# Head-by-head query scores and early best-sixteen lists in a retention, sparse-attention and expert-lookup layer, with gate products from the 24th expert block

## The reference

```python
q = (xt @ wq).reshape(n, 8, 2, 128)                 # 8 heads, 2 sides
s = einsum('nhpd,pkd->nhpk', q, subkeys)            # 128 scores for each head and side
sv, si = top_k(s, 16)
cand = sv[:, :, 0, :, None] + sv[:, :, 1, None, :]  # 16 x 16 sums
cs, ci = top_k(cand.reshape(n, 8, 256), 16)
eidx, gate = ..., softmax(cs)                       # 16 experts of a head, of 128*128
hid = gelu(einsum('cd,chkd->chk', x, u[eidx]))
out = einsum('chk,chkd->cd', gate * hid, v[eidx])
```

## Time and profile before

| | us |
|---|---|
| median of 3 runs (1794.49 to 1795.36) | 1794.93 |
| the profiled execution, its span | 1793.2 |
| TensorE busy in the span | 1774.3 (99%) |
| VectorE busy | 1388.5 (77%) |
| ScalarE busy | 766.7 (43%) |
| GpSimd busy | 170.8 (10%) |

### The profile page before, as it was taken

One profiled execution on the slowest core, in us unless ns is written; L12 is line 12 of the kernel. 1 busy time (PEld: TensorE's weight loads), 2 busy tenths in 40 slices (PEclk: granted clock), 3 DMA queues, 4 the chain that ended last, 5 costly groups with the idle time before them and its releaser, 6 DMA issues.

```text
span 1793.2 us, 27943 instructions
## 1 busy us (share of the span) xinstructions
PE 1774.3 (99%) x10680; PEld 1591.7 (89%) x10680; DVE 1388.5 (77%) x2153; ACT 766.7 (43%) x1054; POOL 170.8 (10%) x158
## 2 busy tenths in 40 slices
PE   8999999999999999999999999999999999999998
PEld 8899989789999999999977777789999998777775
DVE  6546667566459796888378898989999998898996
ACT  5334444655331010111155555555555555555555
POOL 0000000000000121222100000111111111111010
PEclk9999999999999999999999999999999999999999
DMA  9774544556545987998999899999999999999984
GB/s 351 262 280 149 165 141 142 188 187 226 187 150 192 358 333 282 342 336 331 362 377 361 317 324 341 344 350 367 377 369 374 377 347 361 353 359 365 357 309 152
DMA packets 77275, 531.01 MB, mean 296 GB/s; under 512 B 8811, under 2 KB 9211, under 8 KB 16268
## 3 DMA queue, kind: packets, MB, share of 16 engines
q1 hardware_dynamic: 54512, 377.96, 56.6%
q0 software_dynamic: 22352, 151.59, 23.2%
q10 hardware_dynamic: 332, 0.44, 0.1%
HBM read 512.60 MB, written 15.20 MB: 294 GB/s over the span
## 4 chain that ended last, share of the span: by engine, by line
PE 97%; DVE 1%; issue 1%; ACT 1%; DMA 0%; DVEq 0%; SPq 0%; ACTq 0%
PE bank L918 19%; PE bank L934 11%; PE bank L596 8%; PE bank L597 8%; PE bank L598 8%; PE bank L1015 6%; PE bank L1014 6%; PE bank L1019 6%; PE bank L1021 6%; PE bank L1020 6%; PE bank L935 5%; PE bank L973 2%; PE bank L743 0%; PE bank L952 0%; PE bank L791 0%
## 5 line engine op out<-in xcount | busy, mean ns | idle before, releaser
L1932 DVE TENSOR_TENSOR lo<-raw,hi 128x1024 fp32r<-128x1024 f32 x384 | 463.6, 1221 | 101.7 <-ACT hi L1318 101.3
L1318 ACT ACTIVATE hi<-raw 128x1024 fp32r<-128x1024 f32 x384 | 404.9, 1059 | 320.8 <-PE bank L1021 233.5
L918 PE MATMUL bank<-hT,raw 128*128 128x192 f32 x2048 | 337.4, 326 | 0.0
L918 PEld LDWEIGHTS bank<-hT,raw 128*128 128x128 f32 x2048 | 332.3, 190 | 0.1
L934 PE MATMUL bank<-xr,hi 128*128 128x384 f32 x1024 | 291.3, 359 | 0.0
L935 PE MATMUL bank<-xr,lo 128*128 128x192 f32 x1024 | 256.3, 250 | 0.0
L1444 DVE TENSOR_TENSOR lo<-raw,hi 128x2048 fp32r<-128x2048 f32 x75 | 171.8, 2290 | 103.7 <-ACT hi L1086 68.2
L1015 PE MATMUL bank<-lo,wm 128*64 128x512 f32 x512 | 202.8, 396 | 0.0
L1014 PE MATMUL bank<-hi,wm 128*128 128x512 f32 x512 | 199.9, 390 | 1.7 <-DVE wm L1987 1.2
L1019 PE MATMUL bank<-lo,wm 128*128 128x512 f32 x512 | 200.3, 391 | 0.0
L1021 PE MATMUL bank<-hi,wm 128*128 128x512 f32 x512 | 199.3, 389 | 0.0
(11 more groups left out here) (293 smaller groups left out, 2686.2 us busy)
## 6 DMA issues: line engine op xcount, KB each, us to landing
raw<-in_u SPq DMA_DIRECT2D x128, 1024.0 KB, 7.7
raw<-in_v SPq DMA_DIRECT2D x128, 1024.0 KB, 7.2
raw<-in_w_in SPq DMA_DIRECT2D x43, 1024.0 KB, 5.8
raw<-in_w_out SPq DMA_DIRECT2D x16, 1024.0 KB, 4.8
raw<-in_wq SPq DMA_DIRECT2D x16, 1024.0 KB, 4.8
gate_matrix<-gs POOLq DMA_DIRECT2D x12, 768.0 KB, 12.5
gs<-gate_matrix SPq DMA_DIRECT2D x12, 768.0 KB, 9.2
raw<-in_cmp_w SPq DMA_DIRECT2D x8, 1024.0 KB, 4.8
```

The costliest lines, as they stand in the source:

```text
L918: last = mm(bank[s % 2][:, 0:TD], raw[:, s, k * P:(k + 1) * P], xn[:, k, 0:TD], start=(k == 0), stop=(k == KT - 1))
L1318: do(hi[:, s % 2, cols], raw[:, s, cols], ACT.Copy).then_inc(v_hi_ready, 1)
L1932: vec.tensor_tensor(lo[:, n % 2, cols], raw[:, n % RAW, cols], hi[:, n % 2, cols].bitcast(F32), ALU.subtract).then_inc(v_lo_ready, 1)
```

## The change

**Scores.** `query_scores(h)` makes the four products of one head (both sides, both halves of the tokens) behind block 2h + 2 of the query stage, into bank 2 or 3. Heads 0 to 6 are made there, head 7 behind `u` block 0, where all eight were. ScalarE copies a head's scores with one instruction, `copy_scores(h)`, behind its rounding of block 2h + 4.

**Lists.** `early_list()` makes one list at a time. VectorE does 20 of them (heads 0 to 4, both sides, both halves) in the query stage: one in block 4, two in each of the blocks 5 to 11, one in each of the blocks 12 to 15, and one more behind them. `route_tokens` keeps the lists of heads 5 to 7.

**Gates.** `ROUTED` goes from 32 to 24: TensorE waits for the choices after `u` block 23, gate products lie in the blocks 25 to 48, 24 expert columns are gated at once and 104 are stored, in 13 groups. The first 14 items are let through from block 9 on and are shared over 13 parts of tt = 0 (before: 18), the next 24 lie in the blocks 24 to 59 (before: 32 to 59).

**Places.** `sc` moves to `gs`, the sums and the wide passes to `arena`, the lists to a tile `top_sb` of their own. The loops over the query blocks are written out on TensorE, ScalarE and VectorE.

```diff
-ROUTED = 32
+ROUTED = 24
+EARLY_HEADS = 5
...
-EXP_SPARSE, EXP_DENSE, PAIRS_LISTED = 10, 27, 13
+EXP_SPARSE, EXP_DENSE, PAIRS_LISTED = 7, 20, 9
...
+            def query_scores(h):
+
+                if h == 0:
+                    pe.wait_ge(decay_loaded, 32)
+                if h >= 2:
+                    pe.wait_ge(q_copied, h - 1)
+                pe.wait_ge(acc_evacuated, M_WQ + 2 * h + 2)
+                for tt in range(2):
+                    for s in range(2):
+                        g, to = 2 * h + s, (2 * tt + s) * P
+                        last = mm(bank[2 + h % 2][:, to:to + P], qT[:, g * T + tt * P:g * T + (tt + 1) * P], subk[:, s, :], start=True, stop=True)
+                last.then_inc(q_scores, 1)
+
+            for b in range(2, KT):
+                weights_block(M_WQ + b, b, x=h_parts)
+                if b % 2 == 0:
+                    query_scores(b // 2 - 1)
...
+            for b in range(RAW, KT):
+                rest_block(M_WQ + b, b, b % RAW)
+                if RAW < b < KT - RAW:
+                    early_list()
+                scaled(M_WQ + b - 1, b - 1, qT[:, (b - 1) * T:b * T])
+                if b >= KT - RAW:
...
+                early_list()
+            while done["lists"] < 4 * EARLY_HEADS:
+                early_list()
+            scaled(M_PEER - 1, 1, qT[:, (KT - 1) * T:KT * T])
...
-                total = PH + PH // 2 + 6
+                total = PH - EARLY_HEADS + PH // 2 + 6
...
-                for x in range(PH):
+                for x in range(EARLY_HEADS, PH):
                     g = 2 * x
-                    dv.wait_ge(q_copied, 4 * (1 - tt) + x // 2 + 1)
+                    dv.wait_ge(q_copied, x + 1)
```

More of the change, by code:

```diff
@@ L217, in build @@
         choiceT = at("choiceT", 50432, [P, 3, T])
+        top_sb = at("top_sb", 49152, [P, 2, 512])
         base = at("base", 51200, [P, 3 * P + 3 * TS])
@@ L944, in _ @@
                 if r == 0:
[L945 to L954, removed]
+                    query_scores(PH - 1)
             with pe.Fori(1, ROUTED // RAW) as lap:
@@ L1298, in pair_gelus @@
                     do(cols, cols, ACT.Gelu_apprx_tanh).then_inc(hcol_ready, 1)
[L1300 to L1303, removed]
+            for h in range(PH - 2, PH):
+                copy_scores(h)
             ac.wait_ge(res_stored, 16)
@@ L1758, in _ @@
                 normalise((0, 8)[s - 2], (8, KT)[s - 2])
[L1759 to L1774, removed]
+            done = {"route": 0, "items": 0, "lists": 0}
             def step(ins):
@@ L1783, in routed, with best16, early_list @@
                 dv.wait_ge(route, done["route"])
+            def best16(vals, idx, src):
+                for v, l in zip(vals, src):
+                    step(vec.max(v[:, 0:8], l))
+                routed()
+                for v, x, l in zip(vals, idx, src):
+                    step(vec.max_index(x[:, 0:8], v[:, 0:8], l))
+                routed()
+                for v, l in zip(vals, src):
+                    step(vec.match_replace(l, v[:, 0:8], l, LOWEST))
+                routed()
+                for v, l in zip(vals, src):
+                    step(vec.max(v[:, 8:16], l))
+                routed()
+                for v, x, l in zip(vals, idx, src):
+                    step(vec.max_index(x[:, 8:16], v[:, 8:16], l))
+                routed()
+            def early_list():
+                n = done["lists"]
+                done["lists"] += 1
+                h, tt, s = n // 4, 1 - n % 4 // 2, n % 2
+                g = 2 * h + s
+                dv.wait_ge(q_copied, h + 1)
+                best16([top[:, tt, g, :]], [top_i[:, tt, g, :]], [sc[:, tt, g, :]])
+            for b in range(RAW, KT):
+                rest_block(M_WQ + b, b, b % RAW)
[3 more added lines that the diff above has]
+                if b >= KT - RAW:
+                    if b == KT - RAW:
+                        dv.wait_ge(sparse_loaded, 16)
+                        dv.wait_ge(rstd_ready, 3)
+                    s = b - KT + RAW
+                    cols = slice(s * 512, (s + 1) * 512)
+                    vec.scalar_tensor_tensor(out=xs[TS:P, cols], in0=h_sparse[:, cols], scalar=rstd_cols[TS:P, 1:2], in1=g2_row[TS:P, cols],
+                                             op0=ALU.mult, op1=ALU.mult).then_inc(xs_ready, 1)
+                early_list()
+            while done["lists"] < 4 * EARLY_HEADS:
+                early_list()
+            scaled(M_PEER - 1, 1, qT[:, (KT - 1) * T:KT * T])
             def pair_item():
```

45 lines of the change are left out of this document (12 added, 33 removed).

## The result

| | kernel before | changed kernel |
|---|---|---|
| median, us | 1794.71 (1794.22 to 1795.36, 4 runs) | 1813.67 (1812.42 to 1814.47, 4 runs) |
| span of the profiled execution, us | 1793.2 | 1812.0 |

The ratio is 1.0105, with a 95% interval of 1.0093 to 1.0116: the changed kernel is slower by 19 us. Forecast were 14.8 us and a time of 1809.7; the measured time lies inside the range, 1801 to 1817, and the other side of the forecast (TensorE waits for the choices) came about. The 4.2 us between forecast and loss are mainly two terms: a wait 2.6 us longer, and 2.1 us behind it that the sum did not have. The sum's 0.4 us for the first `v` stage did not come about.

What follows compares the result with a forecast made beforehand. TensorE, busy 99% of the span, was taken as the bound. To the median of 1794.9 us came 14.4 us of waiting for the choices, 0 for the query stage and 0.4 for the first `v` stage: 1809.7 us, range 1801 to 1817.

Steps and rivals of the forecast that it cites:

- 0.4 us for the first `v` stage: First `v` stage: eight more blocks gated just ahead of use cost TensorE 0.4 us, bounds 0 and 4.1.
- TensorE arrives at the transposes: End of `u` block 23: TensorE reaches the transposes of the choices at about 648.0 us.
- cost of the query stage: Query stage: VectorE's early lists fit beside the blocks, so TensorE waits 0 us, bounds 0 to 3.7.
- pairs leave: End of the tt = 1 lists: pairs leave for GpSimd at 569.0 us, 14.9 us earlier than before.
- item 0 / item 2 / item 7: VectorE's gathered tiles in tt = 0: multiplications start at 579.6, 591.6 and 625.7 us.
- item 11 / item 13: Last gathered tiles: two row buffers yield one per 6.0 us; item 13 starts at 659.3 us.
- choices ready: End of VectorE's routing: 3.1 us from the last tile's start to the choices, at 662.4 us.
- wait: Ahead of the transposes: TensorE stands 14.4 us for the choices; 9 to 22 us expected, chance 72%.
- the landing of the last gathers: Gathers ahead of the choices: 8.9 us from issue to multiplication, the last about 6.5 us without weight loads.
- The forecast by the Trainium skill's rule: Gathers at an estimated 4.4 us per 1 MB: stall about 4.5 us, time 1800; the prediction went by the rows instead.
- The rival of an overrun: Query stage: single lists of 2.1 us make VectorE overrun, 3.7 us more, 1813.4 us; chance 7%.
- The signs: Expected in the trace: VectorE idle some 7 us before its first tile, query blocks 5.76 and 6.65, choices 24 to 27 earlier.
- The choices come in time: At the choices: added gather waits shrink under 3 us, TensorE does not stand, 1794.9 to 1798 us; chance 7%.

Runs made afterwards that it cites:

- experiment 1: Changed kernel with ROUTED back at 32 and the exponentials and pair lists at their old values, leaving head-by-head scores and early lists: 1794.47 us, ratio 1.0.
- experiment 5: Changed kernel with a third row buffer for the first fourteen gathered tiles and the last two of them multiplied behind the choices: 1794.90 us, ratio 1.0001.
- experiment 7: Changed kernel with 140 more transposes of a constant tile, results unused, on TensorE ahead of its wait for the choices: 1810.78 us.
- experiment 2: Kernel before with only the gates moved to block 24 and the exponentials to blocks 10 and 23, no early lists: 1831.51 us, one run.
- experiment 8: Kernel of experiment 1 with two more searches, results overwritten, ahead of each of the twenty early lists: 1805.95 us, ratio 1.0063.
- two tiles behind: Changed kernel with the last two of the fourteen gathered tiles multiplied behind the choices, all gathers left in place: 1804.85 us, ratio 1.0051.
- experiment 3: Changed kernel with a third row buffer for the first fourteen gathered tiles, nothing else changed: 1804.15 us, ratio 1.0052.

## Why the prediction was right, point by point

The mechanism, its place and its sign were right. The size was 4.2 us short, and by luck no more: VectorE's lead of 1.4 us at item 7 and the 0.4 us for the `v` stage, both misjudged, worked against the two errors below. Without them 6.0 us would have been missing. What each step gave:

| step | forecast, us | measured, us |
|---|---|---|
| TensorE arrives at the transposes | 648.0 | 648.0 (665.02 - 17.01) |
| single list in the query stage | 1.82 | 1.83 |
| cost of the query stage | 0 | 0 (experiment 1) |
| pairs leave | 569.0 | 568.3 |
| item 0 / item 2 / item 7 | 579.6 / 591.6 / 625.7 | 578.5 / 589.6 / 624.3 |
| item 11 / item 13 | 649.7 / 659.3 | 651.0 / 661.9 |
| choices ready | 662.4 | 665.0 |
| wait | 14.4 | 17.0 |
| lower clock behind the wait | not in the sum | 2.1 |
| first `v` stage | 0.4 | 0 (experiment 5) |

- **The mis-sized term is the landing of the last gathers**, and it is the whole of the 2.6 us. Up to item 7 VectorE was even 1.4 us ahead of the forecast; 0.7 us of that is where the pairs left, since the 14.9 us taken over from before held a wait of 0.87 us for the exponential that is gone in the changed kernel. From item 7 to item 11 it took 6.7 us an item, not 6.0, with landings of 10.0 and 10.3 us where the step used 8.9, that of the last gather before. In the kernel before, six of the fourteen products had waited for their gather, and two of these landings took 9.9 and 10.8 us, so 8.9 rested on one row of several. That turned 1.4 us of lead into 1.3 us of delay. The last landing was taken as 6.5 us, the fastest of the earlier trace rows, because no weights would be loaded; it took 7.8. That is 1.3 us more. This landing varies from one kernel to the next: 5.3 us in experiment 7, where TensorE had ended its last `u` block at about the same time, and in experiment 2, where TensorE stands three times, the median of the stretch is 6.9. So 6.5 lay within what it does, but as the one fastest row it was too favourable a value for the sum. The bounds of 9 to 22 us held.
- **The missing term is the clock.** The prediction said "with 5.2 us blocks on both sides" of the wait. Behind it two blocks took 11.62 us. The rows read of before show no stand between two stretches of full work, so no row had the price, but a term with a bound of its own belonged there: the first instructions behind the stand at half the clock. Experiment 7 shows it to be a consequence of the stand.
- **The forecast by the Trainium skill's rule** ("DMA: Bandwidth & Descriptors", "Anatomy of one DMA — SWDGE (gpsimd) path": 2 us and the bytes over 436 GB/s, by estimate 4.4 us for 1 MB) was a stall of 4.5 us and 1800 us. The landings of the changed kernel were 6.9 us at the least, 9.6 in the median, with weight loads on the same engines, and the shortest read in any run here was 5.3; the measurement decides.
- **The query stage** was forecast to hold with 0.8 to 1 us in hand. `lo` of block 12 was ready at 495.9 and needed at 497.5, 1.6 us. The rival of an overrun was sound in kind: experiment 8 made the lists dearer, and TensorE waited almost for every bit of it.
- **The first `v` stage.** The same stretch, now 19 us later, can be held against the earlier trace rows:

```profile
1066.00:1103.00 37.00, 36.90 (x162) 28.07 (x161) 34.45 (x55) 20.90 (x32) 3.59 (x3) 1.00 0.94 341
```

  TensorE is busy for 36.90 of 37 us (before: 36.88) beside VectorE at 34.45. Its waits there for the gated weights are 1.2 us in all before and after, and the first `v` block was already 18.8 us late when it began (919.7 against 900.9), the whole difference of the spans.
- **The signs.** VectorE stood 7.1 us ahead of its first gathered tile and 0.8 to 3.2 us ahead of each of the last six, as said, and query blocks came 5.76 and 6.65 us apart. The choices came 21.8 us earlier than 686.8 and not 24 to 27, by the 2.6 us above. "The choices come in time" needed the added waits for gathers to shrink from 17.5 us to under 3. Experiment 5 is that case made by hand, and it gave what the rival said: 1794.9.

The loss by stands, where each was measured. The sum is the stand, what the clock cost behind it and, for the two tiles behind, 0.6 us of waiting for one-hots:

| kernel | stand, us | behind it, us too long | sum | span less 1793.2 |
|---|---|---|---|---|
| changed | 17.0 | 2.1 | 19.1 | 18.8 |
| third buffer | 7.4 | 3.1 | 10.5 | 10.5 |
| both edits | 0 | 0 | 0 | 0.1 |
| two tiles behind | 6.9 | 2.1 | 9.6 | 10.2 |
| gates alone | 27.6 in three | 9.4 in three | 37.0 | 36.5 |

(Too long is measured against six transposes and two blocks at the full clock, 0.66 + 10.40 = 11.06 us; for the stands of "gates alone" as given in experiment 2.)

## What to carry to other kernels

Moving a meeting point of two engines forward pays only as far as the slower side can follow. List what that side does up to the point, and separate its work (here 75.9 us, which would have fitted) from the loop of transfers that feeds it, which keeps its own pace, landing plus reissue over the number of buffers; when the work shrinks, that loop becomes the bound. More buffers or fewer transfers ahead of the point moved it here; that cheaper work would not was argued from the waits and not tried. And move all that the earlier point depends on: in experiment 1 one exponential left in its old place gave back most of what the early lists had gained. And where TensorE is 99% busy, such a change can at best be free: the version that removed the whole wait was level with the kernel before.

## What the runs showed of the hardware

- A stand of TensorE costs more than its length. The granted clock was 0.50 behind one of 17 us, and 2.1 us were lost there; 3.1 us behind one of 7.4 us; 2.1 us behind one of 6.9 us; 3.1 to 3.2 us behind each of the three of 5.7, 6.5 and 15.4 us in experiment 2; 1.95 us behind one of only 2.1 us, at 0.53. In these the extra did not shrink with the length of the stand, so the short one nearly doubled. With 15.45 us of otherwise useless transposes in the stand (0.8 us of it was left), the clock stayed at 1.00.
- The same gather, 128 rows of 8 KB, the last ahead of the choices, took 5.3, 7.8 and 11.5 us in experiment 7, the changed kernel and experiment 3. Of all in the stretch the longest was 11.0 us with two buffers and 12.7 with three; the medians were alike, 9.6.
